# FFN down projection of a streaming encoder step: from plain tiles to seven block products, with token blocks kept in DRAM

## The chip, the cores and the metric

One core of a Trainium2 chip runs the kernel. The metric is the device time of one execution in microseconds (us), lower is better. Matrix products run on TensorE (PE; its weight loads are shown as PEld), elementwise work on VectorE (DVE), ScalarE (ACT) and GpSimd (POOL); SyncE (SP) issues most transfers between DRAM and the on-chip memory.

## The reference

A trunk of two layers over 1,152 tokens (1,024 of a prompt, 128 of eight sample sequences), model width 1,024. Each layer has mixers and then a SwiGLU FFN of width 2,816. All is float32. What matters here:

```
h = rms_norm(x, norm_ffn_w[layer]) * (1.0 + sc_f) + sh_f
x = x + g_f * ((jax.nn.silu(h @ w_gate[layer]) * (h @ w_up[layer])) @ w_down[layer])
# x (T, 1024), w_gate and w_up (1024, 2816), w_down (2816, 1024); g_f by sequence
```

The rest of the trunk (the projections, RWKV-7, Mamba-2 and HGRN2 mixers, the final norm) isn't touched.

## The kernel before

Activations lie transposed: x is `g.xT`, 128 partitions of model dimension by 8 tiles by T = 1,152 tokens. Tokens are cut in three chunks of CH = 384. Hidden units come in KF = 22 tiles of 128. To keep float32 accuracy every operand of a product is split into a high part (`...H`) and a low remainder (`...L`), and each product is three matmuls: high by high, high weights by low tokens, low weights by high tokens.

`ffn` has two stages, and `Mixed` (L1157) carries the first. It makes the tiles of gate and up for one unit tile j as a 2x2 block product: two output tiles (gate, up) and two halves of the 8 input tiles (HALF = 4) for weights, against two halves of the input and two token chunks (0 and 1). Seven products replace eight: each has its own sum of weight blocks (A11, A12, S1, S2, S4, A22, S3, A21, made on POOL in `sums` and `differences`) and its own sum of token blocks. The token blocks B11, B21, T1, T2, B22, T3, T4 lie split in `BH` and `BL` all the time and serve every group. Chunk 2 (with the samples' tokens, `hH` and `hL`) is done plainly: the four "far" products.

A group j runs so. SP loads weights into `g.raw` (`load1`, `load2`; each waits for POOL's use of the room in the group before). ACT copies the high part of one weight block at a time into one of SLOTS = 4 slots of `WH` when PE has left the slot (`act_ahead`, `act_second`, `act_group`), POOL subtracts it for the low part into `WL` (`low`, L1217), and PE (`pe_group`, L1334) goes through far, B11, far, B21, T1, T2, B22, far, T3, T4, far, four input tiles by three matmuls each. PSUM results are copied by ACT (`take_p1`, `take_u2`, `take_u3`), added by DVE (`add_c11`, `add_c12`, `take2`, `take_far`), weighted by the norm, silu on ACT, multiplied on DVE (`multiply`), and the unit tile of hidden is stored to DRAM (`store`, 576 KB).

The down stage is plain. Units come in six parts (2, 4, 4, 4, 4, 4 tiles). `load_hidden` brings a unit tile back from DRAM, ACT (`split_hidden`, L1731) and DVE (`low_hidden`, L1768) split it into the half of `BH` and `BL` that the part before doesn't use, so the next part is made ready while this one runs. For each part and each of the 8 output tiles PE does units x 3 x 3 matmuls (L1704); POOL splits the weights (L1674, L1676), and DVE adds the tile to `xT` (L1777 to L1786), in the last part with its squares for the next norm (L1791, L1793).

The order on every engine is the order in the text of its block; an engine that waits holds all that stands behind it. SP's queue, too, is in order: loads of a group, then the store of the unit before.

Of the kernel before, what the change touches and what calls it, by code (L numbers as in the profile page):

```python
# [15 lines left out]
F32 = mybir.dt.float32  # L16
# [5 lines left out]
P = 128  # L22
# [1130 lines left out]
B11, B21, T1, T2, B22, T3, T4 = range(7)  # L1153
# [3 lines left out]
class Mixed:  # L1157
# [10 lines left out]
    def __init__(self, nc, g, ph, layer, which, groups, out1, out2, room, room2, tail=True):  # L1168
        self.nc, self.g, self.N, self.out, self.tail, self.sq = nc, g, groups, (out1, out2), tail, room2[:, 0:T]
# [10 lines left out]
        self.sc, self.sh = g.scale[:, layer, which, :, :], g.modcol(layer, 3 * which)  # L1180
        self.A11, self.A12, self.A21, self.A22 = (
            g.raw[:, n, k * HALF:(k + 1) * HALF, :] for n in range(2) for k in range(2))
# [9 lines left out]
        (self.p1_mm, self.p2_mm, self.p5_mm, self.p6_mm, self.p3_mm, self.p7_mm, self.p4_mm, self.far1a_mm, self.far1_mm,  # L1192
         self.far2b_mm, self.far2_mm) = ph.sems("p1_mm p2_mm p5_mm p6_mm p3_mm p7_mm p4_mm far1a_mm far1_mm far2b_mm far2_mm")
# [7 lines left out]
    def load1(self, sp, j, src):  # L1201
        if j == 0:
            return
        sp.wait_ge(self.s3_set, j)
        sp.dma_start(self.g.raw[:, 0], src).then_inc(self.raw1_in, 16)

    def load2(self, sp, j, src):
        if j:
            sp.wait_ge(self.s3_set, j)
            sp.wait_ge(self.a21_lo, j)  # L1210
        sp.dma_start(self.g.raw[:, 1], src).then_inc(self.raw2_in, 16)
# [3 lines left out]
    def low(self, pool, slot, src, hi, n, lo):  # L1215
        pool.wait_ge(hi, n)
        self.nc.gpsimd.tensor_tensor(self.WL[:, slot], src, self.WH[:, slot].bitcast(F32), ALU.subtract).then_inc(lo, 1)  # L1217

    def sums(self, pool, j):
        tt, S = self.nc.gpsimd.tensor_tensor, self.S  # L1220
        pool.wait_ge(self.raw2_in, 16 * (j + 1))
        if j:
            pool.wait_ge(self.s3_lo, j)
        tt(S[:, 0], self.A21, self.A22, ALU.add).then_inc(self.s1_set, 1)
        pool.wait_ge(self.s1_set, j + 1)
        if j:
            pool.wait_ge(self.s4_lo, j)
        tt(S[:, 1], S[:, 0], self.A11, ALU.subtract).then_inc(self.s2_set, 1)

    def differences(self, pool, j):  # L1230
        tt, S = self.nc.gpsimd.tensor_tensor, self.S
        pool.wait_ge(self.s2_lo, j + 1)
        tt(S[:, 1], self.A12, S[:, 1], ALU.subtract).then_inc(self.s4_set, 1)
        pool.wait_ge(self.s1_lo, j + 1)
        tt(S[:, 0], self.A11, self.A21, ALU.subtract).then_inc(self.s3_set, 1)
# [8 lines left out]
    def pool_first(self, pool):  # L1244
        low, S = self.low, self.S
        pool.wait_ge(self.first_in, self.first)
        low(pool, 2, self.A11, self.a11_hi, 1, self.a11_lo)
        low(pool, 3, self.A12, self.a12_hi, 1, self.a12_lo)
        self.nc.gpsimd.tensor_tensor(self.diffs[0], self.g.xT[:, 0:HALF, 0:CH], bc(self.sc[:, 0:HALF, 0], 2, CH), ALU.mult
                                     ).then_inc(self.diff_half, 1)  # L1250
        low(pool, 0, self.A22, self.a22_hi, 1, self.a22_lo)
        low(pool, 1, self.A21, self.a21_hi, 1, self.a21_lo)
# [7 lines left out]
    def pool_group(self, pool, j):  # L1260
        low, S = self.low, self.S
        pool.wait_ge(self.raw1_in, 16 * j)
        low(pool, 2, self.A11, self.a11_hi, j + 1, self.a11_lo)
        low(pool, 3, self.A12, self.a12_hi, j + 1, self.a12_lo)
        self.sums(pool, j)
        low(pool, 0, S[:, 0], self.s1_hi, j + 1, self.s1_lo)
        low(pool, 1, S[:, 1], self.s2_hi, j + 1, self.s2_lo)
        self.differences(pool, j)
        low(pool, 2, S[:, 1], self.s4_hi, j + 1, self.s4_lo)
        low(pool, 3, self.A22, self.a22_hi, j + 1, self.a22_lo)  # L1270
        low(pool, 0, S[:, 0], self.s3_hi, j + 1, self.s3_lo)
        low(pool, 1, self.A21, self.a21_hi, j + 1, self.a21_lo)
# [3 lines left out]
    def product(self, slot, bank, x, start=True, stop=True, n=CH, before=None):  # L1276
        for k in range(HALF):
            if before:
                before(k)
            for w, lows in ((self.WH, (0, 1)), (self.WL, (0,))):  # L1280
                for low in lows:
                    ins = self.nc.tensor.matmul(self.acc[:, bank, 0:n], w[:, slot, k, :], x(low, k),  # L1282
                                                start=start and k == 0 and w is self.WH and low == 0,
                                                stop=stop and k == HALF - 1 and w is self.WL, skip_group_check=True)
# [5 lines left out]
    def far(self, slot, bank, half, first, before=None):  # L1290
        return self.product(slot, bank, lambda low, k: (self.hH, self.hL)[low][:, half * HALF + k, 0:CH + SHIFTS],
                            start=first, stop=not first, n=CH + SHIFTS, before=before)
# [12 lines left out]
    def pe_first(self, pe):  # L1305
# [6 lines left out]
        far(2, BFAR1, 0, True, before=lambda k: pe.wait_ge(self.h_lo, k + 1)).then_inc(self.far1a_mm, 1)  # L1312
# [21 lines left out]
    def pe_group(self, pe, j):  # L1334
        mixed, far = self.mixed, self.far
        pe.wait_ge(self.a11_lo, j + 1)
        pe.wait_ge(self.far1_out, j)
        far(2, BFAR1, 0, True).then_inc(self.far1a_mm, 1)
        pe.wait_ge(self.u3_copied, j)
        mixed(2, BX, B11, stop=False).then_inc(self.p1_mm, 1)  # L1340
        pe.wait_ge(self.a12_lo, j + 1)
        far(3, BFAR1, 1, False).then_inc(self.far1_mm, 1)
        pe.wait_ge(self.c21_done, j)
        mixed(3, BY, B21).then_inc(self.p2_mm, 1)
        pe.wait_ge(self.s1_lo, j + 1)
        pe.wait_ge(self.c22_done, j)
        mixed(0, BZ, T1).then_inc(self.p5_mm, 1)
        pe.wait_ge(self.s2_lo, j + 1)
        pe.wait_ge(self.p1_copied, j + 1)
        mixed(1, BX, T2, start=False, stop=False).then_inc(self.p6_mm, 1)  # L1350
        pe.wait_ge(self.s4_lo, j + 1)
        pe.wait_ge(self.c12_done, j)
        mixed(2, BV, B22).then_inc(self.p3_mm, 1)
# [2718 lines left out]
```

## Time and profile before

| | us |
|---|---|
| median of 3 runs (3846.08 to 3853.86) | 3851.03 |
| the profiled execution, device time | 3851.7 |
| its span | 3850.0 |
| PE busy (93%) | 3582.3 |
| POOL busy (37%) | 1415.3 |
| DVE busy (55%) | 2132.8 |
| ACT busy (27%) | 1046.7 |

In the timeline of the whole span the FFN of layer 0 goes from about 1317 to 2134 us and that of layer 1 from 3016 to 3822. The mean granted clock of TensorE is 0.964 of its full speed. Matmul rows overlap in time (a matmul is shown from its start to its modelled end), so the distance of two starts is what one costs; some instructions of SP and PE's sequencer are not shown as busy. In a timeline, `[x <-Y]` behind a row is the idle time before it and what ended it. A number behind x is how many instructions a row merges. Engine names with q are queues: SPq rows are DMA issues.

### The profile page before, as it was taken

To read this page: it belongs to the slowest core of one execution; us is meant where nothing else is said; L and a number is where in the kernel's file an instruction comes from. 1 tells how busy PE (TensorE), PEld (TensorE's weight loads), DVE (VectorE), ACT (ScalarE), POOL (GpSimd) and SP (SyncE) were. 2 spreads that over 40 slices of the span, in tenths; PEclk is the share of its full clock that TensorE was granted. 3 is DMA by queue.
4 is the path that set the end of the run, shared out by engine and by line. 5 is a ranking of instruction groups with operands and counts; after the bars stand their busy time and mean duration, and the time that the engine had idled before them with its cause. 6 is when DMAs were issued, how large, how long until landed. Compare 5 with 4: busy or idle time off the path is not lost. (4 is left out here: it accounts for less than half of the span.)

```text
span 3850.0 us, 69479 instructions
## 1 busy us (share of the span) xinstructions
PE 3582.3 (93%) x29720; PEld 3377.8 (88%) x29720; DVE 2132.8 (55%) x3046; ACT 1046.7 (27%) x1720; POOL 1415.3 (37%) x1137
## 2 busy tenths in 40 slices
PE   7999978888989899999999999978868899999998
PEld 6999967777659899999999999977758799999998
DVE  5543655664884764545545544346665855555445
ACT  2000125552641143333100232024430433332100
POOL 5222221120003377777432322220003577776331
PEclk8999989998999999999999999989979999999999
DMA  6455541002331022222322233232231122222321
GB/s 213 164 180 174 175 106 31 22 22 64 75 102 43 28 69 74 69 75 69 124 91 60 65 111 120 83 102 84 74 117 48 39 75 70 73 74 95 108 85 72
DMA packets 393189, 339.26 MB, mean 88 GB/s; under 512 B 19683, under 2 KB 363233, under 8 KB 386766
## 3 DMA queue, kind: packets, MB, share of 16 engines
q1 hardware_dynamic: 381568, 290.89, 24.9%
q10 hardware_dynamic: 11214, 44.33, 2.9%
q8 instruction: 214, 3.51, 0.4%
q0 software_dynamic: 128, 0.00, 0.2%
q14 instruction: 65, 0.53, 0.0%
HBM read 249.95 MB, written 85.24 MB: 87 GB/s over the span
## 5 line engine op out<-in xcount | busy, mean ns | idle before, releaser
L1282 PE MATMUL ffn_acc<-ffn_BH,ffn_WH 128*128 128x384 f32 x1232 | 417.9, 339 | 22.9 <-DVE ffn_BL L1487 15.1
L1282 PE MATMUL ffn_acc<-ffn_BL,ffn_WH 128*128 128x384 f32 x1232 | 416.3, 338 | 0.0
L1282 PE MATMUL ffn_acc<-ffn_BH,ffn_WL 128*128 128x384 f32 x1232 | 415.6, 337 | 0.0
L1217 POOL TENSOR_TENSOR ffn_WL<-raw,ffn_WH 128x512 fp32r<-128x512 f32 x176 | 282.4, 1606 | 260.2 <-ACT ffn_WH L1368 260.2
L1704 PE MATMUL ffn_acc<-ffn_BH,ffn_WH 128*128 128x384 f32 x1056 | 353.8, 335 | 7.2 <-DVE ffn_BL L1768 4.5
L1704 PE MATMUL ffn_acc<-ffn_BL,ffn_WH 128*128 128x384 f32 x1056 | 353.4, 335 | 0.0
L641 PE MATMUL in_ab_acc<-hH,in_ab_wH 128*128 128x384 f32 (+2 forms) x840 | 288.7, 344 | 7.2 <-DVE hL L502 7.2
L1217 POOL TENSOR_TENSOR ffn_WL<-ffn_S,ffn_WH 128x512 fp32r<-128x512 f32 x176 | 278.5, 1593 | 27.4 <-ACT ffn_WH L1368 27.4
L641 PE MATMUL in_ab_acc<-hL,in_ab_wH 128*128 128x384 f32 (+2 forms) x840 | 285.0, 339 | 0.0
L641 PE MATMUL in_c_acc<-hH,in_c_wH 128*128 128x384 f32 (+1 forms) x768 | 260.6, 339 | 6.8 <-DVE hL L502 6.8
L641 PE MATMUL in_c_acc<-hL,in_c_wH 128*128 128x384 f32 (+1 forms) x768 | 260.6, 339 | 0.0
L1282 PEld LDWEIGHTS ffn_acc<-ffn_BH,ffn_WH 128*128 128x128 f32 x1232 | 233.5, 190 | 28.7 <-POOL ffn_WL L1217 13.9
L1282 PE MATMUL ffn_acc<-ffn_hH,ffn_WH 128*128 128x394 f32 x704 | 241.7, 343 | 7.0 <-DVE ffn_hL L1519 6.1
L1282 PE MATMUL ffn_acc<-ffn_hH,ffn_WL 128*128 128x394 f32 x704 | 242.1, 344 | 0.0
L1282 PE MATMUL ffn_acc<-ffn_hL,ffn_WH 128*128 128x394 f32 x704 | 242.0, 344 | 0.0
L1704 PE MATMUL ffn_acc<-ffn_BH,ffn_WL 128*128 128x384 f32 x1056 | 240.4, 335 | 0.0
L1777 DVE SCALAR_TENSOR_TENSOR xT<-ffn_acc,mod,xT 128x768 f32<-128x768 f32 x96 | 97.6, 1017 | 254.1 <-PE ffn_acc L1704 253.9
L1282 PEld LDWEIGHTS ffn_acc<-ffn_BL,ffn_WH 128*128 128x128 f32 x1232 | 233.9, 190 | 0.4
L1282 PEld LDWEIGHTS ffn_acc<-ffn_BH,ffn_WL 128*128 128x128 f32 x1232 | 233.8, 190 | 0.0
L1704 PEld LDWEIGHTS ffn_acc<-ffn_BH,ffn_WH 128*128 128x128 f32 x1056 | 198.7, 188 | 8.4 <-DVE ffn_BL L1768 5.1
L1704 PEld LDWEIGHTS ffn_acc<-ffn_BL,ffn_WH 128*128 128x128 f32 x1056 | 198.8, 188 | 0.0
L641 PE MATMUL in_ab_acc<-hH,in_ab_wL 128*128 128x384 f32 (+2 forms) x840 | 196.2, 338 | 0.0
(624 smaller groups left out, 8257.5 us busy)
## 6 DMA issues: line engine op xcount, KB each, us to landing
in_ab_ada<-in_ada_w SPq DMA_DIRECT2D x40, 1024.0 KB, 5.0
hidden<-ffn_up SPq DMA_DIRECT2D x44, 576.0 KB, 2.8
raw<-in_w_gate SPq DMA_DIRECT2D x44, 512.0 KB, 3.8
raw<-in_w_up SPq DMA_DIRECT2D x44, 512.0 KB
raw<-in_w_down SPq DMA_DIRECT2D x80, 256.0 KB, 2.7
pT<-in_ab_out ACTq DMA_DIRECT2D x34, 576.0 KB, 3.3
pT<-in_c_out ACTq DMA_DIRECT2D x32, 576.0 KB, 3.7
raw<-in_w_in_ab SPq DMA_DIRECT2D x34, 512.0 KB, 4.7
```

The source lines that it names most:

```text
L641: ins = self.nc.tensor.matmul(self.acc[0:rows, u, c, 0:n], w[:, u, k, 0:rows], x[:, k, c * CH:c * CH + n], start=(k == 0 and w is self.wH ...
L1217: self.nc.gpsimd.tensor_tensor(self.WL[:, slot], src, self.WH[:, slot].bitcast(F32), ALU.subtract).then_inc(lo, 1)
L1282: ins = self.nc.tensor.matmul(self.acc[:, bank, 0:n], w[:, slot, k, :], x(low, k), start=start and k == 0 and w is self.WH and low == 0, s ...
L1704: ins = nc.tensor.matmul(acc[:, pair + c if c < 2 else third, 0:CH], w[:, slot, k, :], x[:, k, chunk(c)], start=k == 0 and w is m.WH and x ...
L1777: stt(xs, acc[:, pair:pair + 2, 0:CH], gate[:, n, 0:1], xs, ALU.mult, ALU.add)
```

## The change

The down stage, too, is done by `Mixed`'s seven block products. A weight block is now 128 output columns by half of the units of a part (the even or the odd unit tiles), the two output tiles are a pair of model tiles. Units come in three parts of 4, 4 and 3 pairs of tiles. A part has four groups (one per pair of output tiles), so groups 22 to 33 (G = 34) follow the 22 groups of gate and up in the same loops; a group of the last part has blocks of three tiles instead of four (`halves`).

The token blocks of a part are made of hidden, so they change with the part. `multiply` leaves the even unit's tile in `g.sumsq` (`even`) and the odd one's in `up`, four differences of 384 columns are made per pair on DVE, and nine blocks of 128x384 per pair (B11, FAR_0, T1; B21, B22, FAR_1; T3, T2, T4; 192 KB each) are stored to DRAM instead of two tiles. Before each part all its blocks are loaded back (`load_units`) through four rooms of one tile (RING), copied by ACT to their places in `BH` or `hH` (`take_units`) as soon as the last group of the part before has used a place, and subtracted by DVE (`low_units`). They stand between the other work of these engines: B11, B21, T1, T2 and FAR_1 in the last group of the old part, FAR_0, B22, T3 and T4 in the first group of the new one. PE waits for each block (`fresh`).

In `pe_group` the first two far products now come behind B21 and in the order FAR_1, FAR_0. Weights are loaded in two DMAs per half instead of one. The diff, cut:

```
+    def load(self, sp, n, j, src, loaded):
+        for k in range(2):
+            sp.dma_start(self.g.raw[:, n, k * HALF:k * HALF + self.halves[j]], src(k)).then_inc(loaded, 16)
...
-    def pe_group(self, pe, j):
+    def pe_group(self, pe, j, n=CH + SHIFTS, fresh=lambda name: None):
         pe.wait_ge(self.a11_lo, j + 1)
-        pe.wait_ge(self.far1_out, j)
-        far(2, BFAR1, 0, True).then_inc(self.far1a_mm, 1)
-        pe.wait_ge(self.u3_copied, j)
-        mixed(2, BX, B11, stop=False).then_inc(self.p1_mm, 1)
-        pe.wait_ge(self.a12_lo, j + 1)
-        far(3, BFAR1, 1, False).then_inc(self.far1_mm, 1)
-        pe.wait_ge(self.c21_done, j)
-        mixed(3, BY, B21).then_inc(self.p2_mm, 1)
+        pe.wait_ge(self.u3_copied, j)
+        mixed(2, BX, B11, stop=False, h=h, before=fresh(B11)).then_inc(self.p1_mm, 1)
+        pe.wait_ge(self.a12_lo, j + 1)
+        pe.wait_ge(self.c21_done, j)
+        mixed(3, BY, B21, h=h, before=fresh(B21)).then_inc(self.p2_mm, 1)
+        pe.wait_ge(self.far1_out, j)
+        far(3, BFAR1, 1, True, n=n, h=h, before=fresh(FAR_1)).then_inc(self.far1b_mm, 1)
+        far(2, BFAR1, 0, False, n=n, h=h, before=fresh(FAR_0)).then_inc(self.far1_mm, 1)
...
     def act_group(self, act, j, free1, refill=lambda act, j, n: None):
...
         self.take_p1(act, j)
+        refill(act, j, 0)
+        act.wait_ge(self.far1_mm, j + 1)
         act.wait_ge(self.s4_set, j + 1)
-        high(2, S[:, 1], self.s4_hi)
-        act.wait_ge(self.far1_mm, j + 1)
+        high(2, S[:, 1, 0:h], self.s4_hi)
         act.wait_ge(self.p2_mm, j + 1)
+        high(3, self.A22[j], self.a22_hi)
+        refill(act, j, 1)
...
+        high(1, self.A21[j], self.a21_hi)
+        refill(act, j, 2)
...
+FRESH = (B11, B21, T1, T2, FAR_1, FAR_0, B22, T3, T4)
+RING = 4
...
-    parts = (2, 4, 4, 4, 4, 4)
+    N, NQ = KF, KF // 2
+    parts = (4, 4, 3)
...
+            def load_units(p, name):
...
+                for i in range(parts[p]):
+                    u = first_unit(p, name) + i
+                    if u >= RING:
+                        sp.wait_ge(u_lo, u - RING + 1)
+                    sp.dma_start(unit_room[:, u % RING, :], g.hidden[name, first_q[p] + i]).then_inc(u_in[u % RING], 16)
+            load2(0)
+            for j in range(G):
+                p = before_part(j)
+                if p is not None:
+                    load_units(p, B11)
+                    load_units(p, B21)
+                load1(j + 1)
+                if p is not None:
+                    load_units(p, T1)
+                    load_units(p, T2)
+                    load_units(p, FAR_1)
+                load2(j + 1)
+                if p is not None:
+                    load_units(p, FAR_0)
+                    load_units(p, B22)
+                if j < N:
+                    store(j)
+                if p is not None:
+                    load_units(p, T3)
+                    load_units(p, T4)
...
+            def refill(act, j, place):
+                p = before_part(j)
+                if p is not None and place == 0:
+                    take_units(p, B11, m.p1_mm, j + 1)
+                if p is not None and place == 1:
+                    take_units(p, B21, m.p2_mm, j + 1)
+                if p is not None and place == 2:
+                    take_units(p, T1, m.p5_mm, j + 1)
+                    take_units(p, T2, m.p6_mm, j + 1)
+                    take_units(p, FAR_1, m.far2b_mm, j + 1)
+            def refill_rest(j):
+                p = before_part(j - 1)
+                if p is not None:
+                    take_units(p, FAR_0, m.far2_mm, j)
+                    take_units(p, B22, m.p3_mm, j)
+                    take_units(p, T3, m.p7_mm, j)
...
             m.act_first(act)
-            for j in range(1, N):
+            for j in range(1, G):
                 if j > 1:
                     m.act_ahead(act, j)
...
+                else:
+                    take_u3(j - 1)
+                    m.act_second(act, j)
+                refill_rest(j)
+                m.act_group(act, j, free1, refill_last)
...
+            for j in range(1, G):
+                p, last = before_part(j), before_part(j - 1)
...
+                if last is not None:
+                    low_units(last, FAR_0)
+                    low_units(last, B22)
+                    low_units(last, T3)
                 m.add_c11(dve, j)
+                if last is not None:
+                    low_units(last, T4)
+                if p is not None:
+                    low_units(p, B11)
+                m.take_far(dve, j, 0) if j < N else add_far(j, 0)
+                if p is not None:
+                    low_units(p, B21)
                 m.add_c12(dve, j)
+                if p is not None:
+                    low_units(p, T1)
+                m.weigh1(dve, j) if j < N else add_near(j, 0)
+                if p is not None:
+                    low_units(p, T2)
                 m.take2(dve, j)
+                if p is not None:
+                    low_units(p, FAR_1)
+                m.weigh2(dve, j) if j < N else add_near(j, 1)
+                m.take_far(dve, j, 1) if j < N else add_far(j, 1)
+                if j < N:
+                    multiply(j)
```

`take_units` waits for PE's use of the old block and for each landing, then copies; `low_units` waits for each copy. `add_near` and `add_far` are the adds of a pair of tiles to `xT`, from the block sums and from PSUM.

## Rows read from the trace of the kernel before

**Rows 1.** Windows: us, then PE, PEld, DVE, ACT, POOL busy, clock, DMA share, GB/s.
```profile
1364.00:1851.90 487.90, 487.20 (x2771) 486.89 (x2770) 255.79 (x322) 162.14 (x277) 369.09 (x254) 1.00 0.22 72
1851.90:2131.50 279.60, 275.32 (x1587) 274.57 (x1585) 147.33 (x228) 23.13 (x20) 85.12 (x94) 1.00 0.29 87
...
3060.00:3539.50 479.50, 478.80 (x2723) 478.48 (x2722) 247.79 (x312) 158.24 (x271) 361.68 (x250) 1.00 0.23 73
3539.50:3819.30 279.80, 276.90 (x1586) 275.98 (x1584) 147.40 (x229) 23.05 (x20) 86.04 (x94) 0.99 0.28 85
```

**Rows 2.** Timeline of PE in the down stage: start, us, instruction.
```profile
2119.04 0.33 PE L1704 MATMUL ffn_acc<-ffn_BH,ffn_WH 128*128 128x384 f32 x1
...
2119.91 0.33 PE L1704 MATMUL ffn_acc<-ffn_BL,ffn_WH 128*128 128x384 f32 x1
```

**Rows 3.** Timeline of DVE at the start of one gate group.
```profile
1504.12 0.56 DVE L1572 TENSOR_TENSOR ffn_up<-ffn_acc,ffn_rstd 128x384 f32<-128x384 f32 x1 [0.60 <-PE ffn_acc L1282]
```

**Rows 4.** Timeline of POOL in the same group.
```profile
1504.64 1.29 POOL L1224 TENSOR_TENSOR ffn_S<-raw 128x512 f32<-128x512 f32 x1
...
1507.25 3.57 POOL L1217 TENSOR_TENSOR ffn_WL<-ffn_S,ffn_WH 128x512 fp32r<-128x512 f32 x2
...
1513.46 1.28 POOL L1217 TENSOR_TENSOR ffn_WL<-ffn_S,ffn_WH 128x512 fp32r<-128x512 f32 x1
...
1519.67 1.88 POOL L1217 TENSOR_TENSOR ffn_WL<-raw,ffn_WH 128x512 fp32r<-128x512 f32 x1 [0.54 <-ACT ffn_WH L1368]
```

**Rows 5.** Timelines of PE and of DVE at the start of group 1.
```profile
1363.60 0.41 PE L1282 MATMUL ffn_acc<-ffn_hH,ffn_WH 128*128 128x394 f32 x1 [0.45 <-DVE ffn_bias L1573]
...
1368.11 0.54 DVE L1563 TENSOR_TENSOR ffn_up<-ffn_up,ffn_acc 128x384 f32<-128x384 f32 x1
```

**Rows 6.** Timeline of DVE at a tile of the last part.
```profile
2127.45 1.36 DVE L1791 TENSOR_TENSOR ffn_sq<-xT 128x1152 f32<-128x1152 f32 x1
2128.84 1.36 DVE L1793 TENSOR_TENSOR sumsq<-sumsq,ffn_sq 128x1152 f32<-128x1152 f32 x1
```

**Rows 7.** DMA issues, down stage from 1860 to 2120, then the whole span: KB each, us to landing.
```profile
raw<-in_w_down SPq DMA_DIRECT2D x40, 256.0 KB, 2.7
...
raw<-in_w_down SPq DMA_DIRECT2D x3, 128.0 KB, 2.2
...
ffn_gated<-hidden SPq DMA_DIRECT2D x20, 576.0 KB, 3.8
...
raw<-in_w_down SPq DMA_DIRECT2D x16, 128.0 KB, 3.7
```

**Rows 8.** Timeline of ACT in the gate group of rows 3.
```profile
1506.01 0.62 ACT L1368 CAST ffn_WH<-ffn_S 128x512 fp32r<-128x512 f32 x1 [3.42 <-POOL ffn_S L1224]
...
1518.91 0.62 ACT L1368 CAST ffn_WH<-raw 128x512 fp32r<-128x512 f32 x1 [1.14 <-PE ffn_acc L1282]
```

**Rows 9.** Splits into ffn_BH and ffn_BL: ns min, median, max.
```profile
L1731 ACT CAST ffn_BH<-ffn_gated x20: 1156/1163/1167, 1861.7 to 3733.1; 128x1152 fp32r<-128x1152 f32 x20
L1768 DVE TENSOR_TENSOR ffn_BL<-ffn_gated,ffn_BH x20: 1344/1346/1631, 1862.9 to 3752.8; 128x1152 fp32r<-128x1152 f32 x20
...
L1494 DVE TENSOR_TENSOR ffn_BL<-ffn_up,ffn_BH x12: 944/949/959, 1340.1 to 3044.3; 128x768 fp32r<-128x768 f32 x12
```

**Rows 10.** Timeline of DVE: one add beside POOL, and without.
```profile
1504.78 1.29 DVE L1576 TENSOR_TENSOR ffn_up<-ffn_up,ffn_bias 128x128 f32<-128x128 f32 x1
...
1852.98 0.29 DVE L1576 TENSOR_TENSOR ffn_up<-ffn_up,ffn_bias 128x128 f32<-128x128 f32 x1
```

**Rows 11.** Timeline of SP's queue in the group of rows 3.
```profile
1509.70 0.34 SPq L1637 DMA_DIRECT2D hidden<-ffn_up  x1
```

**Rows 12.** PE's first matmul after the down stage, and windows of 3 us there.
```profile
2138.51 0.66 PE L641 MATMUL in_c_acc<-hH,in_c_wH 128*128 128x384 f32 x1 [6.82 <-DVE hL L502]
...
2138.00:2141.00 3.00, 2.49 (x8) 2.52 (x9) 3.00 (x4) 3.00 (x4) 1.24 (x1) 0.50 0.72 193
2141.00:2144.00 3.00, 3.00 (x16) 3.00 (x15) 3.00 (x2) 3.00 (x4) 2.92 (x3) 0.78 0.00 0
```

## What the change is expected to do to the time

> **What bounds the kernel now.** I read the windows by stage first, then PE's starts in time, then one group on ACT, POOL, DVE and SP. In both FFNs PE is all but full: the groups of gate and up (1364 to 1851.9 us, 3060 to 3539.5) have it busy for 487.2 of 487.9 and 478.8 of 479.5 us, the down stage (1851.9 to 2131.5, 3539.5 to 3819.3) for 275.3 of 279.6 and 276.9 of 279.8 [rows 1]. The reader is to see there that DVE and ACT have room on average and that POOL is the next engine (369 of 488 us). The price of a matmul is not its row's 0.33 us (they overlap) but the distance of starts: 0.87 us for five, 0.1734 us each [rows 2]. 1,584 matmuls (8 tiles x 22 units x 3 chunks x 3 products) are 274.7 us, so the down stage idles some 5.0 us per layer.
>
> **What the change takes away.** A down product over pairs becomes seven block products and four far ones: 33 matmuls per pair of units and pair of tiles. Parts of 4, 4 and 3 unit pairs, four tile pairs each: 4 x 11 x 33 = 1,452 matmuls for 1,584, so 132 x 0.1734 = **22.9 us less per layer**. The 5.0 us of idle time end with the old stage: **27.9 less**.
>
> **Inside the groups.** A group of gate and up takes 23.2 us (487.9 us hold 21 [rows 1]) and one began at 1503.9 or so: DVE's take of the last far product stands at 1504.12 [rows 3]. Twelve matmuls are 2.08 us. POOL's sums start 0.7 us into it, the low half of S4 ends at 10.8 [rows 4], and B22 wants it at 12.7. So a down group with four units, without switches, holds PE's pace: the same twelve POOL instructions, no silu, less on DVE. With three units both shrink by a quarter. I cost it at nothing, covered by this lead of 1.9 us; the cover shrinks in odd gate groups, where DVE now makes three differences of 384 columns beside POOL. Between 0 and 0.5 us for each of 11 groups: I take 0.5 us per layer. The added stores (nine blocks of 192 KB a pair, for two of 576 KB) go out on SP behind hidden_done; the load behind them waits for POOL's S3 anyway, so they cost nothing here.
>
> The new order of PE (far products after B21) moves a wait forward: B21 of group 1 wants c21_done 2.08 us after the group's start at 1363.60, so at 1365.7, and DVE ends it at 1368.65 [rows 5]; before it was wanted at +6.4. The memset ahead of it on DVE leaves. Bounds 0 and 3.0, I take **2 us** per layer. At the end DVE now squares tile 6 after the last product: one square and one sum, 1.36 us each, less the wide add of 1.0 that now lies before PE's end: **1.7 us** [rows 6].
>
> **The switches: the new cost.** Before each of the three parts, 36 blocks (27 in the last) of 128x384 come back from DRAM by a ring of four rooms; each is loaded by SP, copied by ACT, its low half made by DVE, and only then is its room loaded again. No row shows a block, but near ones do. Landing: 2.2 us for 128 KB, 2.7 for 256 KB, 3.8 for 576 KB [rows 7], so 2.45 for 192 KB. ACT: 0.62 us for 512 columns [rows 8], 1.16 for 1152 [rows 9], so 0.5. DVE: 0.95 for 768 and 1.35 for 1152 [rows 9], so 0.55. A room's turn is about 3.6 us, and twelve blocks in a row some 11. Add the hold: the same DVE add of 128x128 takes 1.29 us while POOL works and 0.29 without [rows 10], and two POOL subtractions took 3.57 us where one alone takes 1.28 [rows 4]. So a low half beside POOL costs DVE up to 1.8 us a block, and POOL 0.5.
>
> The engines' queues put this on the path twice. With t = 0 at the start of the last group before part 1 (four units):
> (a) *Ahead of the next A11.* ACT takes T1, T2 and FAR_1 at the end of its group, before act_ahead. B21's low halves are done at 15.4 (POOL's holds between), T1's, behind add_c12 (third product at 14.6, u2 copied at 15.9), at 20.0; T2 lands 21 to 22.5, FAR_1 24.1 to 26.1 and is copied at 26.6. Then A11's copy (0.6) and POOL (1.3): the next group starts at 28.5, not 22.9. 5.6 us late; 2.8 if no DVE instruction meets POOL. Now A11's copy comes right behind the third product [rows 8].
> (b) *Ahead of S1.* refill_rest (FAR_0, B22, T3: twelve blocks) stands ahead of act_group. FAR_1's low halves wait for take2, hence for u3, which ACT copies after A11: 34.4. FAR_0 comes after two adds on DVE: 37.0, wanted at 34.7 (2.3 late). B22 lands by 41.3, T3 by 45.2, is copied at 45.7; S1's copy and low half end at 47.6, and PE had been through FAR_0 at 39.1: 8.5 late. POOL's next four instructions with T4's holds end at 54, two products after T1 end at 51.8: 2.2 late.
> Sum 18.6; with all holds and queues free 9; I take **17**, since POOL is dense there [rows 4]. Behind the waiting ACT stand the weight copies, behind those POOL, behind POOL PE: nothing runs ahead.
> Part 0 has more: SP's four B11 loads stand behind the store of unit 20, at 7.5 (the store of before left at +5.8 [rows 11]), which holds S4's copy (2 us); (a) 5.3; FAR_1 1; FAR_0's low halves wait behind unit 21's multiply and three differences, at about 42.9 for 37.7 (5.2); SP puts six stores ahead of T3, so S1 is at 54.4 for 44.9 (9.5); POOL 2. **25**, bounds 16 and 30. Part 2 has nine blocks where there are twelve, so the ring runs one ahead: (a) 1.9, (b) 6.8 and 1.2: **10**, bounds 6 and 14. **52 us per layer**; lowest 31, highest 64, and 78 if each of five landings in a row takes 1 us more, as the down weights did at the switch of before (128 KB: 3.7 us as the median of those in the page, 2.2 later) [rows 7].
>
> **The clock.** After 6.8 us without PE work the granted clock was 0.50 of full (1.2 of 2.4 GHz) and its mean from 2141 to 2144 was 0.78, so PE ran at half until about 2142.3, some 4 us from its start at 2138.5 [rows 12]: 2 us lost. Each switch has a stall of that length, but the products behind it wait for POOL anyway: 0 to 8 us per layer, I take 4.
>
> **Sum** per layer: -27.9 + 52 + 4 + 0.5 + 2 + 1.7 = +32.3; two layers +65. The profiled execution took 3851.7 us (span 3850.0), 0.7 over the median, so **3916 us**.
>
> **Rivals.** *Hidden refills, faster.* If the engines' other work covers the blocks (they are loaded while PE still runs the old part), a switch costs its weight chain only, some 5 us: -27.9 + 15 + 2 = -11 per layer, 3830. It decides below 8 us a switch. For it: units preloaded before the group ends, SP idle. Against it: twelve copies stand ahead of A11 and twelve ahead of S1, and three ring turns in a row don't fit in the 8.3 us from third product to group end. The Trainium skill (DMA: Bandwidth & Descriptors, "Rules for kernel authors") advises to issue a DMA early and wait late, since its fixed cost overlaps; by that this rival would hold. It needs rooms to issue into, and four are full after four blocks. Chance 0.09.
> *No holds.* The switches at 31 to 42 a layer, clock and holds at nothing: -27.9 + 31 + 2 = +5 to -27.9 + 42 + 2 = +16, so 3862 to 3884. Chance 0.21, the lowest tip of it within the bound of measurement.
> *Holds and landings in full.* 78 a layer and 8 for the clock: -27.9 + 78 + 8 + 4 = +62: up to 3976. For it: the two adds [rows 10]. Chance 0.2. The Trainium skill (SBUF — State Buffer, the shared port pair) says of a VectorE instruction with two SBUF inputs and a GpSimd one that the second fully blocks until the first ends. The trace agrees (1.29 for 0.29 us); by it every low half beside POOL would be stretched, which is this case.
> *Forecast:* 3884 to 3950, chance 0.5.
>
> **How the numbers follow.** The range 3868 to 3975 leaves out the faster case, the lowest part of the second and the end of the third. 0.2% is 7.7 us, about what a measurement can tell: faster 0.09, same 0.04, slower 0.87.
>
> **What would show it.** In the trace after: copies into ffn_BH from ffn_sq, 128x384, 198 in all and their u_lo waits; in three places per layer two PE gaps, the first ending with POOL's low half of A11, the second with that of S1, 3 to 6 and 7 to 10 us; FAR_0's gap at the first switch from DVE; matmuls 0.1734 us apart else; groups of 22.9 and 17.2 us between switches. Wrong if PE has no gap over 2 us at the switches (then 3830), or if the plain down groups idle too (then over 3975).

## The result, and the profile after

The changed kernel took 3940.39 us as the median of four runs (3938.56 to 3948.25), the kernel before 3850.39 beside it (3846.08 to 3853.86): ratio 1.0239, 95% interval 1.0226 to 1.0251, 90 us more, or 45.0 per layer. The profiled execution has a span of 3939.0 us.

The page after, the costliest form of the block products, two DMA issues, and one line of the table of waits (us in total, times, longest):

```profile
L1290 PE MATMUL ffn_acc<-ffn_BH,ffn_WH 128*128 128x384 f32 x1848 | 640.0, 346 | 123.4 <-POOL ffn_WL L1225 95.6
...
ffn_sq<-hidden SPq DMA_DIRECT2D x198, 192.0 KB, 2.5
...
hidden<-ffn_up SPq DMA_DIRECT2D x110, 192.0 KB, 2.0
...
PEld ffn_acc L1290 <- POOL ffn_WL L1225: 117.9, 36, 10.4
```

The 198 block loads are there, at 2.5 us each. PE's idle time is ended by POOL's low halves of the weights (L1225), 95.6 of 123.4 us of this form. Where the idle time lies is told by PE's timeline. These are the rows with idle time over 2 us from the last gate group to the end of the down stage in layer 0, but for one more like those at 2127.59 and 2148.05 (start, us, instruction, idle time before it):

```profile
1847.81 0.69 PE L1290 MATMUL ffn_acc<-ffn_BH,ffn_WH 128*128 128x384 f32 x1 [3.18 <-POOL ffn_WL L1225]
...
1865.49 0.66 PE L1290 MATMUL ffn_acc<-ffn_BH,ffn_WH 128*128 128x384 f32 x1 [4.16 <-POOL ffn_WL L1225]
...
1876.58 0.44 PE L1290 MATMUL ffn_acc<-ffn_hH,ffn_WH 128*128 128x384 f32 x1 [2.19 <-DVE ffn_hL L1845]
...
1889.91 0.69 PE L1290 MATMUL ffn_acc<-ffn_BH,ffn_WH 128*128 128x384 f32 x1 [9.94 <-POOL ffn_WL L1225]
...
1981.85 0.69 PE L1290 MATMUL ffn_acc<-ffn_BH,ffn_WH 128*128 128x384 f32 x1 [6.03 <-POOL ffn_WL L1225]
...
2000.16 0.69 PE L1290 MATMUL ffn_acc<-ffn_BH,ffn_WH 128*128 128x384 f32 x1 [7.41 <-POOL ffn_WL L1225]
...
2087.84 0.45 PE L1290 MATMUL ffn_acc<-ffn_BH,ffn_WH 128*128 128x384 f32 x1 [2.16 <-POOL ffn_WL L1225]
...
2102.14 0.69 PE L1290 MATMUL ffn_acc<-ffn_BH,ffn_WH 128*128 128x384 f32 x1 [6.19 <-POOL ffn_WL L1225]
...
2127.59 0.44 PE L1290 MATMUL ffn_acc<-ffn_BH,ffn_WH 128*128 128x384 f32 x1 [2.20 <-POOL ffn_WL L1225]
...
2148.05 0.44 PE L1290 MATMUL ffn_acc<-ffn_BH,ffn_WH 128*128 128x384 f32 x1 [2.20 <-POOL ffn_WL L1225]
...
2185.17 0.66 PE L641 MATMUL in_c_acc<-hH,in_c_wH 128*128 128x384 f32 x1 [8.55 <-DVE hL L502]
```

At each of the three switches PE waits for POOL at A11 and at S1 (4.16 and 9.94, 6.03 and 7.41, 2.16 and 6.19 us). At the first it waits for DVE at FAR_0 (2.19), and before the first for S4 in the last gate group (3.18). Together these are 41.3 us. The three plain groups of three units have 2.20 each. The last row answers to 6.82 before [rows 12].

ACT's timeline at the first switch shows what held S1's copy (the last row, merged with S2's): ahead of it stand the copies of FAR_0, B22 and T3, twelve blocks, and for the last eight ACT waits three times for the ring's next landing (4.76, 1.34 and 3.58 us):

```profile
1878.97 1.06 ACT L1770 CAST ffn_BH<-ffn_sq 128x384 fp32r<-128x384 f32 x2 [4.76 <-DMA ffn_sq<-hidden]
1881.37 1.05 ACT L1770 CAST ffn_BH<-ffn_sq 128x384 fp32r<-128x384 f32 x2 [1.34 <-DMA ffn_sq<-hidden]
1886.00 1.99 ACT L1770 CAST ffn_BH<-ffn_sq 128x384 fp32r<-128x384 f32 x4 [3.58 <-DMA ffn_sq<-hidden]
1887.90 1.13 ACT L1377 CAST ffn_WH<-ffn_S 128x512 fp32r<-128x512 f32 x2
```

The clock takes a second part. These are two windows from the restart at S1 of the third switch (columns as in rows 1, the granted clock third from the end):

```profile
2102.10:2106.10 4.00, 3.96 (x12) 3.97 (x13) 4.00 (x5) 2.26 (x6) 3.92 (x4) 0.50 0.00 0
2106.10:2110.10 4.00, 4.00 (x24) 4.00 (x24) 2.51 (x6) 1.53 (x4) 4.00 (x5) 0.98 0.34 98
```

Twelve matmuls start in 4 us, then 24: the clock is at half (1.2 GHz) until about 2106. Counted over PE's starts in layer 0 from 1846 to 2120, 109 matmuls stand some 0.32 us apart in place of 0.1734 [rows 2], which costs 16 us. They come in eight runs of 7 to 18, one behind each of the eight gaps.

**Loss by switch.** ACT copies the third product of each tile pair (L1402) once per group, so the distances of these copies give each group's time. Away from switches they are 23.20 us for gate and up, 22.95 for a four-unit group, 20.46 for a plain three-unit one (17.2 without idle time). The one distance that goes from a four-unit to a three-unit group is 18.28 in the kernel without refills (experiment 2). Against these the switches cost 28.9, 18.1 and 12.4 us in layer 0, 59.4 together: 41.3 of idle time, 16 of half clock, and 2 that neither count holds. Layer 1 has 28.3, 18.2 and 12.3.

### The profile page after: what moved, and what is told of

It reads as the page before. It is cut to its first block and busy times, and to the rows that moved or that the text cites. A ratio compares the mean times of both kernels' runs of the same rounds, so it can differ in the third digit from the quotient of the medians.

```text
span 3939.0 us, 70400 instructions
## 1 busy us (share of the span) xinstructions
PE 3576.3 (91%) x29456; PEld 3360.9 (85%) x29456; DVE 2339.3 (59%) x3216; ACT 1227.0 (31%) x2138; POOL 1656.3 (42%) x1233
## 5 line engine op out<-in xcount | busy, mean ns | idle before, releaser
L1290 PE MATMUL ffn_acc<-ffn_BH,ffn_WH 128*128 128x384 f32 x1848 | 640.0, 346 | 123.4 <-POOL ffn_WL L1225 95.6
L1225 POOL TENSOR_TENSOR ffn_WL<-raw,ffn_WH 128x512 fp32r<-128x512 f32 (+1 forms) x272 | 411.5, 1515 | 389.9 <-ACT ffn_WH L1377 389.8
L1225 POOL TENSOR_TENSOR ffn_WL<-ffn_S,ffn_WH 128x512 fp32r<-128x512 f32 (+1 forms) x272 | 417.9, 1547 | 131.7 <-ACT ffn_WH L1377 131.1
L1290 PE MATMUL ffn_acc<-ffn_hH,ffn_WH 128*128 128x394 f32 (+1 forms) x1056 | 361.0, 342 | 10.1 <-DVE ffn_hL L1531 5.3
L1290 PE MATMUL ffn_acc<-ffn_hL,ffn_WH 128*128 128x394 f32 (+1 forms) x1056 | 361.9, 343 | 0.0
L1290 PE MATMUL ffn_acc<-ffn_hH,ffn_WL 128*128 128x394 f32 (+1 forms) x1056 | 361.6, 342 | 0.0
L1377 ACT CAST ffn_WH<-ffn_S 128x512 fp32r<-128x512 f32 (+1 forms) x272 | 164.8, 609 | 481.1 <-POOL ffn_S L1232 195.8
L1377 ACT CAST ffn_WH<-raw 128x512 fp32r<-128x512 f32 (+1 forms) x272 | 164.9, 608 | 305.9 <-PEq L95 131.0
L1290 PEld LDWEIGHTS ffn_acc<-ffn_hH,ffn_WH 128*128 128x128 f32 x1056 | 200.9, 190 | 11.7 <-DVE ffn_hL L1527 6.1
L1290 PEld LDWEIGHTS ffn_acc<-ffn_hH,ffn_WL 128*128 128x128 f32 x1056 | 201.1, 190 | 0.0
L1290 PEld LDWEIGHTS ffn_acc<-ffn_hL,ffn_WH 128*128 128x128 f32 x1056 | 200.5, 190 | 0.0
```

Of the source, the lines that this page charges most:

```text
L1225: self.nc.gpsimd.tensor_tensor(self.WL[:, slot, 0:h], src, self.WH[:, slot, 0:h].bitcast(F32), ALU.subtract).then_inc(lo, 1)
L1377: self.nc.scalar.copy(self.WH[:, slot, 0:src.shape[1]], src).then_inc(hi, 1)
```

## Experiments

Each ran against the kernel before on the same chip (medians 3849.2 to 3850.8).

**1. Order on ACT and DVE alone.** Three kernels move the block copies without changing their number. The first (A11 first):

```diff
                 if p is not None and place == 2:
                     take_units(p, T1, m.p5_mm, j + 1)
-                    take_units(p, T2, m.p6_mm, j + 1)
-                    take_units(p, FAR_1, m.far2b_mm, j + 1)
...
             def refill_rest(j):
                 p = before_part(j - 1)
                 if p is not None:
+                    take_units(p, T2, m.p6_mm, j)
+                    take_units(p, FAR_1, m.far2b_mm, j)
```

`refill_rest` stands behind A11's copy, u3's and A12's.

> Edit: ACT copies only T1 at the end of a part's last group; T2 and FAR_1 come behind A11's copy, u3 and A12's copy of the next group; the rest as changed. Theory (order of the engines' queues): the first gap of each switch (4.2, 6.0 and 2.2 us in layer 0, 7.5, 6.2 and 2.4 in layer 1) goes, u3 comes earlier and with it the low halves of FAR_1, so the ring behind runs some 4 us ahead, but S1 stays behind all blocks: the second gap stays at 6 to 10 us. 3915 us, 3905 to 3925. Rival (the chain of ring turns sets the time of S1, whatever stands before A11): the first gap moves into the second, 3930 to 3940. Rival (bytes of the blocks in the DMA queues): no change beyond 5 us.

The second (S1 first) spreads refill_rest: FAR_0 behind S2's copy, B22 behind A22's, T3 and T4 behind A21's, with DVE's low halves likewise. The third does both.

> Edit: FAR_0 is copied behind S2, B22 behind A22, T3 and T4 behind A21 (DVE's low halves in the like places), so S1 stands behind no block but T2 and FAR_1; the ends of the old part as changed. Theory (order): the second gap (10, 7.4, 6.2 us in layer 0, 9.3, 7.8, 6.1 in layer 1, 47 us) goes with the half-clock stretch behind it, the first stays; small gaps at B22 and T3 of 1 to 2 us may come: 3885 us, 3875 to 3900. Rival (ring turns): PE waits for B22 or T3 in place of S1 for as long, 3930 to 3940.

> Both edits together. Theory (order): both gaps go; what stays are FAR_0's gap at the first switch and waits of 1 to 3 us a switch, plus the shorter groups of the last part: 3840 us, 3830 to 3860. Rival (ring turns): a ring turn is some 3.6 us and seven turns must fit between the old B21 and the new T3, 26 us; they would leave gaps of 5 us a switch: 3865 to 3880. Rival (bytes): over 3900.

They took 3931.49, 3919.08 and 3917.27 us (ratios 1.0211, 1.0173, 1.0170, each +-0.0018). All miss what pure order would give (3915, 3885, 3840). The second and third differ by less than their intervals. In the first kernel A11's gap is gone (what is left at B21 is 0.64 us), but FAR_0 is later for it and S1 hardly less late (5.95 and 9.43 us for 2.19 and 9.94, first switch):

```profile
1865.17 0.41 PE L1290 MATMUL ffn_acc<-ffn_BH,ffn_WH 128*128 128x384 f32 x1 [0.64 <-issue]
...
1876.04 0.69 PE L1290 MATMUL ffn_acc<-ffn_hH,ffn_WH 128*128 128x384 f32 x1 [5.95 <-DVE ffn_hL L1845]
1889.13 0.69 PE L1290 MATMUL ffn_acc<-ffn_BH,ffn_WH 128*128 128x384 f32 x1 [9.43 <-POOL ffn_WL L1225]
```

In the second S1's gap is gone at all three switches, A11 is late by 5.92, 5.91 and 2.15 us, and FAR_0 by 5.70 at the first. In the third neither A11 nor S1 is late, but FAR_0 by 9.97, 4.31 and 4.45 us: its copies stood behind S1's, and that waited for the second half of the weights, which SP loads behind FAR_1's blocks. These are PE at the first switch, then POOL and ACT at the second:

```profile
1876.15 0.69 PE L1290 MATMUL ffn_acc<-ffn_hH,ffn_WH 128*128 128x384 f32 x1 [9.97 <-DVE ffn_hL L1849]
...
1973.71 1.26 POOL L1232 TENSOR_TENSOR ffn_S<-raw 128x512 f32<-128x512 f32 x1 [7.70 <-DMA raw<-in_w_down]
...
1975.07 0.62 ACT L1377 CAST ffn_WH<-ffn_S 128x512 fp32r<-128x512 f32 x1 [2.73 <-POOL ffn_S L1232]
1976.41 0.62 ACT L1377 CAST ffn_WH<-ffn_S 128x512 fp32r<-128x512 f32 x1 [0.72 <-POOL ffn_S L1236]
1976.93 1.75 ACT L1773 CAST ffn_hH<-ffn_sq 128x384 fp32r<-128x384 f32 x4
```

So in these kernels the queue order chose which product waits, and one of them waited in each. Of the 119 us that the switches cost in both layers (experiment 2) order gives back 23.

**2. What the refills cost in all.** The kernel without loads, copies, low halves and PE's waits for them (its down groups multiply the old blocks):

```diff
 def load_units(p, name):
+    return
 def take_units(p, name, used, n):
+    return
 def low_units(p, name):
+    return
-    m.pe_group(pe, j, n=CH, fresh=fresh_of(j))
+    m.pe_group(pe, j, n=CH)
```

> Left out: the loads, copies and low halves of all token blocks and PE's waits for them, so the down groups multiply the old blocks (the down result is another). What the seven products cost with free switches. Theory: the changed kernel less its switch losses (28.9, 18.1, 12.4 us in layer 0 by the periods of u3's copies, 59 a layer, clock included): 3822 us, 3812 to 3832. If it stays above 3850, the blocks aren't the main cause and the plain down groups are.

It took 3820.90 us (ratio 0.9923, 0.9906 to 0.9939). This is 119.5 us under the changed kernel, 59.7 per layer, against the 59.4 read from the trace. What is left of the change is 29 us faster than the kernel before. The plain three-unit groups still take 20.4 us here, so their idle time is not the refills'.

**3. The turn of a room.** Two kernels change it. The first loads half the bytes of each block, the second has eight rooms for four from the second part on (the four more lie in up's spare end and in rstd; the waits and room numbers on SP, ACT and DVE change with them, and only the new tables are shown):

```diff
-sp.dma_start(unit_room[:, u % RING, :], g.hidden[name, first_q[p] + i])
+sp.dma_start(unit_room[:, u % RING, 0:CH // 2], g.hidden[name, first_q[p] + i][:, 0:CH // 2])
```

> Each token block's load brings half of its columns (96 KB for 192; the rest of the room is old, so the down result is another); copies, low halves and waits as changed. Theory (turns of the ring: landing, copy, low half, in the engines' order): a landing of 2.5 us becomes 2.1, some seven turns a switch: 15 us less, 3925, 3915 to 3935. Rival (bytes in the DMA queues): the block loads' share of a switch halves, 3880 to 3900.

```diff
+rooms = [unit_room[:, r, :] for r in range(4)] + [extra] + [m.rstd[:, c * CH:(c + 1) * CH] for c in range(3)]
+room_of = [u % 4 for u in range(n0)] + [u % 8 for u in range(units_to[-1] - n0)]
```

> The changed kernel with eight rooms in place of four from the second part on (the spare end of up and three chunks of rstd), all orders as changed. Theory (both order and turns): loads run eight blocks ahead, so T2 is there early, FAR_1 waits for T1's low half and T3 for FAR_0's: 3 to 4 us off each gap at four of six switches, 28 in all: 3912 us, 3900 to 3922. Rival (order alone, no ring): under 8 us, 3932 or more.

They took 3920.93 and 3911.71 us (ratios 1.0182, 1.0160). In the first a load lands in 2.0 us for 2.5:

```profile
ffn_sq<-hidden SPq DMA_DIRECT2D x198, 96.0 KB, 2.0
```

Half a microsecond per landing gave 19.5 us by the medians, 9.7 per layer, so by an estimate some 19 landings per layer stand in line on the path. The rival of bytes in the queues (3880 to 3900) is out. With eight rooms the first switch, left at four, keeps its 28.8 us, and the second and third fall from 18.1 and 12.4 to 11.5 and 5.3: 13.7 per layer, 28.7 us measured in two. A landing itself took longer there (3.5 us at the median), so the gain is that more loads were on their way at once. PE at the second and third (6.03 and 7.41, 2.16 and 6.19 in the changed kernel; the third's A11 row is gone):

```profile
1979.67 0.45 PE L1290 MATMUL ffn_acc<-ffn_BH,ffn_WH 128*128 128x384 f32 x1 [2.62 <-POOL ffn_WL L1225]
...
1994.85 0.69 PE L1290 MATMUL ffn_acc<-ffn_BH,ffn_WH 128*128 128x384 f32 x1 [5.31 <-POOL ffn_WL L1225]
...
2089.93 0.45 PE L1290 MATMUL ffn_acc<-ffn_BH,ffn_WH 128*128 128x384 f32 x1 [2.73 <-POOL ffn_WL L1225]
```

**4. The plain three-unit groups.** The kernel without the last part's squares and their sums, and the changed kernel with parts of 3, 4 and 4 pairs, which puts the squares into four-unit groups:

```diff
-                if j >= N:
-                    square(j, 0)
-                    square(j, 1)
```

> Left out: the squares and sums of x for the next norm in the last part (the next norm is another). Theory (holds): the groups of three units take 20.5 us and not 17.2 because DVE's four instructions of 1.36 us with two on-chip inputs hold POOL beside them; without them 17.2 us, three groups and two layers make 20 us, and 2.7 us less at each layer's end: 3915 us, 3908 to 3922. Rival (ACT waits 1.9 us there for the weights of the next group, so the loads set the period): 3933 to 3940, only the end is gained.

```diff
-    parts = (4, 4, 3)
+    parts = (3, 4, 4)
```

> The changed kernel with parts of 3, 4 and 4 pairs of units for 4, 4 and 3, nothing else. Theory (squares of the last part stretch POOL's chain past a group of 17.2 us; a switch goes by its blocks): the squares now fall in groups of 22.9 us with a lead of 1.9 us, so the last three groups lose 0 to 1.4 us each for 3.3: 6 to 10 us less per layer; the three groups without a switch in the first part have three units and no squares and lose nothing; the first switch loses some 20 for 28.9, the third 18 for 12.4. Sum about -10 per layer: 3920, between 3910 and 3930. Rival A (a three-unit group is too short for POOL with or without squares): the first part's plain groups take 20.4 us and the time is 3930 or more. Rival B (the squares hold POOL alike in a group of any length): the last groups take 26 us, and the time is about 3935.

They took 3919.79 us (1.0179; 3915 expected) and 3941.72 (1.0233). These are POOL's low halves of S1 and S2, first in the changed kernel and without squares; then in the kernel of 3, 4 and 4, in a three-unit group of the first part, in a four-unit group of the second and in one of the last, with squares:

```profile
2139.73 4.22 POOL L1225 TENSOR_TENSOR ffn_WL<-ffn_S,ffn_WH 128x384 fp32r<-128x384 f32 x2
```

```profile
2133.96 1.99 POOL L1225 TENSOR_TENSOR ffn_WL<-ffn_S,ffn_WH 128x384 fp32r<-128x384 f32 x2
```

```profile
1898.98 1.99 POOL L1225 TENSOR_TENSOR ffn_WL<-ffn_S,ffn_WH 128x384 fp32r<-128x384 f32 x2
...
2042.40 2.55 POOL L1225 TENSOR_TENSOR ffn_WL<-ffn_S,ffn_WH 128x512 fp32r<-128x512 f32 x2
...
2135.07 4.77 POOL L1225 TENSOR_TENSOR ffn_WL<-ffn_S,ffn_WH 128x512 fp32r<-128x512 f32 x2
```

Without squares a three-unit group takes 17.23 us, in either kernel (rival A of the second run is out); with them 20.46, and a four-unit group 24.98 for 22.95. The theory held for the cause; the lead it counted on (1.9 us) did not cover the squares, which cost 2.0 per group there, between theory and rival B. The first switch fell to 23.0 us with its 27 blocks for 36 (20 expected), the third rose to 19.0 (18 expected), and the second to 22.4, which nobody expected. The sum is no gain, 3942 for the 3920 expected.

**5. All together.** The next kernel has both orders of experiment 1, SP's second half of the weights ahead of T2's and FAR_1's blocks, B11's first blocks ahead of the store of unit 20, the squares on ACT, and in group 1 the far products ahead of B21.

> e3_both, and: SP loads the second half of the next weights ahead of T2 and FAR_1 and B11 of the first part ahead of unit 20's store; ACT makes the last part's squares; in group 1 PE does the far products ahead of B21. Theory: e3's gap at FAR_0 (10.3, 4.6, 4.8 us in layer 0) came from S1's sum waiting for weights that SP loaded behind FAR_1; some 3 us a switch goes, 18 in all; half of DVE's holds in the last part go (12), group 1 gives 2.5 a layer, the end 1.4: 3917 less 38, 3880 us, 3865 to 3892. Rival (the ring's turns alone set FAR_0): 3895 to 3905, only squares and group 1 are gained.

It took 3875.22 us (1.0071, 1.0054 to 1.0088), near the 3880 expected, but partly by luck: by the copies' distances, against the third kernel of experiment 1, the switches gave some 12 us for 18 expected and the three-unit groups 17 for 12 (a plain one takes 17.59 us now). FAR_0 is late by 4.57, 2.1 and 0.9 us in layer 0, where it was 9.97, 4.3 and 4.9, as the theory of the weights has it, and B21 by 4.45, 2.87 and 1.99 in its place. PE at the first switch:

```profile
1857.25 0.66 PE L1290 MATMUL ffn_acc<-ffn_BH,ffn_WH 128*128 128x384 f32 x1 [4.45 <-issue]
...
1868.52 0.44 PE L1290 MATMUL ffn_acc<-ffn_hH,ffn_WH 128*128 128x384 f32 x1 [4.57 <-DVE ffn_hL L1874]
```

Then come eight rooms on top, then parts of 3, 4 and 4:

> The kernel of all order changes (3875 us) with eight rooms for the blocks from the second part on, as in the kernel with eight rooms. Theory (the turns of four rooms set what is left at the switches): the eight rooms took 28.7 us off the changed kernel at the second and third switches of both layers; part of that is taken already by the new order, so 15 to 25 us come off here: 3855, between 3850 and 3860. First switch unchanged (a gap of 4 to 5 us at A11 and one at FAR_0 in both layers), no gap over 2 us at the second and third. Rival (what is left at the switches is POOL and DVE holding each other over the low halves, not the rooms): 3870 or more.

> The same with parts of 3, 4 and 4 pairs of units for 4, 4 and 3. Theory (block turns set a switch): the first switch, which alone still goes by four rooms, has 27 blocks for 36 and nine between products for twelve, and gains some 5 us per layer; the third has twelve for nine but eight rooms: 1 to 2 us lost. So 5 to 8 us under the run of 4, 4 and 3: about 3848. Rival (the first switch's loss is the late last gate group, with its stores and its multiply, not the number of blocks): no difference, 3855.

They took 3865.98 us (1.0033, 1.0023 to 1.0042) and 3858.72 (1.0020, 1.0010 to 1.0029). The eight rooms gave 9 us by the medians, 15 by the ratios, where 15 to 25 was expected and 28.7 had come before: part of what they gave was held by something else. The third step is 7 us by the medians and 5 by the ratios, within the 5 to 8 expected. In the last of the three PE is late by 5.48 us at B21 of the second part, which the trace puts down to "issue"; DVE's timeline shows the adds that end c21 at 1941.13, behind low halves that met POOL:

```profile
1941.23 0.66 PE L1290 MATMUL ffn_acc<-ffn_BH,ffn_WH 128*128 128x384 f32 x1 [5.48 <-issue]
```

```profile
1931.10 5.28 DVE L1885 TENSOR_TENSOR ffn_BL<-ffn_sq,ffn_BH 128x384 fp32r<-128x384 f32 x4
1936.31 2.02 DVE L1891 SCALAR_TENSOR_TENSOR xT<-ffn_gated,mod,xT 128x768 f32<-128x768 f32 x1
...
1940.59 0.54 DVE L1583 TENSOR_TENSOR ffn_up<-ffn_up,ffn_acc 128x384 f32<-128x384 f32 x1
```

**6. Fewer and longer low halves.** On that kernel, in the second and third part one DVE instruction for blocks side by side, and take2 ahead of T2's low halves:

```diff
+dve.wait_ge(u_hi, u + b)
+tt(lo, src, hi.bitcast(F32), ALU.subtract).then_inc(u_lo, b - a)
...
-                if p is not None:
-                    low_units(p, T2)
                 m.take2(dve, j)
+                if p is not None:
+                    low_units(p, T2)
```

> The kernel of all order changes, eight rooms and parts of 3, 4 and 4 (3858.7 us) with two edits on DVE: in the second and third part one instruction makes the low halves of all blocks whose rooms lie side by side (four blocks, or one and three) where each block had its own, and the adds that end c21 stand ahead of T2's low halves in every part. In the run before, four low halves beside POOL took 4.2 to 6.0 us and c21 behind them held B21's product by 5.5 and 3.9 us in layer 0. Theory (each DVE instruction pays for meeting POOL, not each column): four blocks in one take 2 to 3 us, both gaps fall under 1 us, some 4 us less per switch at four switches: 3844, between 3838 and 3852, which would be under the kernel before. Rival (the hold goes by the time both engines work, so by columns): a run of four takes 4 us or more, c21's gap goes only by the second edit and comes back as a wait for B21's or FAR_1's low halves: 3855 or more.

It took 3866.08 us (1.0043, 1.0028 to 1.0057), no faster. The theory was right on the instruction and wrong on the time, which is the rival's (3855 or more): four low halves in one took 1.76 us where four had taken 5.28, and c21's gap is gone, but FAR_1's and FAR_0's low halves are late in its place (3.16, then 0.51 and 1.09), and a room is free only when all four are. POOL's pair beside them takes 4.32 us (it was 2.86); the scaling of 768 columns (2.04 us), which the edit brought forward, stands beside its second half. DVE and POOL there:

```profile
1930.68 1.76 DVE L1889 TENSOR_TENSOR ffn_BL<-ffn_sq,ffn_BH 128x1536 fp32r<-128x1536 f32 x1 [2.25 <-ACT ffn_BH L1797]
```

```profile
1931.24 4.32 POOL L1225 TENSOR_TENSOR ffn_WL<-raw,ffn_WH 128x512 fp32r<-128x512 f32 x2 [2.09 <-ACT ffn_WH L1385]
```

How much of the loss is POOL's longer pair and how much the rooms that come free by fours, no run tells apart. No kernel that makes all of the output is under the one before; the best, 3858.72, is 0.2% over it.

## Why the prediction was right, and where its terms were off

3916 was forecast with a range of 3868 to 3975, and slower at 0.87; it came to 3940. Per layer +32.3 was forecast and +45.0 measured.

- **The gain** of 27.9 us (132 matmuls and the old stage's idle time): held. The kernel without refills is 29 us faster than the one before. Twice 27.9 less the three terms below that do not belong to the switches (13.4 in layer 0, 14.7 in layer 1) is 27.7.
- **The switches**, 52 and 4 for the clock: 59.4, near in sum by luck: two errors cancel. Idle time was 41.3 us for 52, at the places named: S4 3.2 for 2; A11 4.2, 6.0 and 2.2 for 5.3, 5.6 and 1.9; FAR_0 of the first 2.2 for 5.2; S1 9.9, 7.4 and 6.2 for 9.5, 8.5 and 6.8. POOL's second lateness after S1 (2.0, 2.2 and 1.2), FAR_1's at the first switch (1) and FAR_0's at the second (2.3) did not come. The bounds of 31 to 64 leave out how the second switch's upper bound was reached; 20 would be needed, where its sum was 18.6. The clock took 16 us for 4: the step "the products behind it wait for POOL anyway" failed. After a gap PE had its inputs and ran its next 7 to 18 matmuls at half rate with no idle time to hide them in. One restart costs what was read before (2 us, [rows 12]; here 1 to 2.8), and there were eight such gaps (the three of 2.20 in the plain groups cost none).
- **Plain three-unit groups**, costed at nothing and forecast at 17.2 us: 9.8 us per layer. This is the step that made most of the miss of 12.7. "With three units both shrink by a quarter" left out the squares, which do not shrink: four DVE instructions of 1.36 us with two inputs [rows 6] beside POOL's sums and low halves. Each met POOL, and POOL's pair took 4.22 us for 1.99 (experiment 4). The rows for it stood ready [rows 4, 10]. The Trainium skill (SBUF — State Buffer, "SBUF: two separate sides") says that such a DVE instruction and a GpSimd one exclude each other for a whole instruction; it was applied to the new low halves and not to the old squares, whose neighbours the change had moved.
- **Group 1**, 2 us with a bound of 3.0: 1.9 in layer 0 and 3.2 in layer 1. From PE's first matmul of group 1 to that of group 2 it is 26.10 us for 24.25 before in layer 0, and 27.46 for 24.25 in layer 1, where eight matmuls ran at half clock besides. PE idles 0.66 us at the group's start and 2.56 at B21; before it idled 0.45 at the start and 0.69 later in the group. c21 ends 1.0 us later than before (1369.68 for 1368.65 [rows 5]): ahead of it on DVE the add of 128 columns took 1.36 us where it had taken 0.29.

```profile
1369.83 0.41 PE L1290 MATMUL ffn_acc<-ffn_BH,ffn_WH 128*128 128x384 f32 x1 [2.56 <-DVE ffn_up L1575]
```

- **The tail**, 1.7 us: 8.55 for 6.82, right. **Odd gate groups**, 0.5: nothing, their distance is 23.20 us as before.
- **Durations**: block copy 0.51 (0.5), low half 0.56 at the median and up to 1.65 (0.55 and 1.8), landing 2.5 (2.45), all from neighbouring rows.

The terms as read from the trace are -27.9 + 59.4 + 9.8 + 1.9 + 1.7 = +44.9 in layer 0 and, in the same way, +45.6 in layer 1, against the 45.0 of the medians. Of the signs, the gaps of the third switch (2.16 and 6.19) fell under the stated 3 to 6 and 7 to 10. Of the rivals, no holds (3862 to 3884) and holds in full (up to 3976) both missed: 63 of the 198 low halves took over 1 us, the others 0.55. Hidden refills is refuted: the DMA could be issued early only into free rooms, and eight rooms gave back 28.7 us. So the advice of the Trainium skill (DMA: Bandwidth & Descriptors, "Rules for kernel authors") to issue early and wait late agrees with these runs, with rooms as its price.

What stays open: why the second switch rose from 18.1 to 22.4 us with parts of 3, 4 and 4. Its last three-unit group is shorter, so the units are due earlier; that fits, but no run tells it apart.

## What to carry to other kernels

A refill through a small ring costs its turns in a row (landing, copy, low half), and moving it in in-order queues mostly chose who was late here (23 of 119 us came back); count the turns that don't fit between two uses, and add a half-rate restart for each long gap that remains. When groups get shorter, list the work on each engine that doesn't shrink with them, and check which of it meets the engine that is next to the bound. Here a saving of 27.9 us per layer didn't pay for data that came back three times per layer at some 20 us each.

## What the runs showed of the hardware

- The same short gap lowered the clock at one place and not at another. After the gap of 2.16 us PE restarted at 2087.84 at full rate, and from 2089.45, 1.6 us later, the starts are 0.32 us apart. After the three gaps of 2.20 in the plain three-unit groups the clock stayed full. After every gap of 4.16 us and more in these stages the first matmul is slow already. PE's rows at the first, then windows of 4 us from the restart there and at 2127.59:

```profile
2089.00 0.33 PE L1290 MATMUL ffn_acc<-ffn_BH,ffn_WH 128*128 128x384 f32 x1
2089.17 0.48 PE L1290 MATMUL ffn_acc<-ffn_BL,ffn_WH 128*128 128x384 f32 x1
2089.45 0.52 PE L1290 MATMUL ffn_acc<-ffn_BH,ffn_WL 128*128 128x384 f32 x1
2089.77 0.52 PE L1290 MATMUL ffn_acc<-ffn_BH,ffn_WH 128*128 128x384 f32 x1
...
2087.84:2091.84 4.00, 4.00 (x16) 4.00 (x17) 4.00 (x5) 0.82 (x2) 3.40 (x3) 0.67 0.26 65
2127.59:2131.59 4.00, 4.00 (x23) 4.00 (x24) 2.31 (x3) 0.84 (x2) 3.97 (x4) 1.00 0.35 99
```

- One DVE instruction of 1536 columns beside POOL took 1.76 us where four of 384 had taken 5.28. POOL's pair beside it went from 2.86 to 4.32, with a second DVE instruction beside it, so about 2 of the 3.5 us stayed saved.
- A load of 96 KB took 2.0 us and one of 192 KB 2.5, so half of the bytes was worth a fifth of a landing. With eight rooms for four a load of 192 KB took 3.5 us at the median.
